# Attention over the memory by head pairs, with query and output pieces in twos

## The reference, cut to what matters

```python
def memory_cross_attention(h, mem_n, w_q, w_kv, w_o, qn, kn):
    q = rms_norm((h @ w_q).reshape(bsz, t, X_HEADS, X_HEAD_DIM), qn)      # 4 heads of 128
    kv = mem_n @ w_kv
    k = rms_norm(kv[..., :D_X].reshape(bsz, m, X_HEADS, X_HEAD_DIM), kn)
    v = kv[..., D_X:].reshape(bsz, m, X_HEADS, X_HEAD_DIM)
    s = jnp.einsum('bqhd,bmhd->bhqm', q, k).astype(jnp.float32) * (X_HEAD_DIM ** -0.5)
    prob = jax.nn.softmax(s, axis=-1).astype(v.dtype)
    o = jnp.einsum('bhqm,bmhd->bqhd', prob, v).reshape(bsz, t, D_X)
    return o @ w_o
```

## Time and profile before

| | before |
|---|---|
| median of 3 runs | 720.66 us (719.37 to 721.8) |
| profiled execution | 718.32 us, span 716.7 us |
| PE busy | 698.8 us, 98% of the span |
| DVE busy | 422.8 us, 59% |
| ACT busy | 308.2 us, 43% |
| chain that ended last | PE 83%, DVE 5%, POOL 4%, DMA 3%, ACT 3% |
| mean granted TensorE clock | 0.998 |

### The profile page before, as it was taken

One profiled execution on the slowest core, in us unless ns is written; L12 is line 12 of the kernel. 1 busy time (PEld: TensorE's weight loads), 2 busy tenths in 40 slices (PEclk: granted clock), 3 DMA queues, 4 the chain that ended last, 5 costly groups with the idle time before them and its releaser, 6 DMA issues.

```text
span 716.7 us, 10845 instructions
## 1 busy us (share of the span) xinstructions
PE 698.8 (98%) x3913; PEld 575.8 (80%) x3913; DVE 422.8 (59%) x711; ACT 308.2 (43%) x514; POOL 131.1 (18%) x134
## 2 busy tenths in 40 slices
PE   8999999999998999999999999999999999999998
PEld 7968887876776787878898888888888887888886
DVE  4997957737664657685856555554555574333333
ACT  5736344467753536253654334334333442332220
POOL 3999974033031110100200000000000000000000
PEclk9999999999999999999999999999999999999999
DMA  9645433167310033011124133232232332231303
GB/s 254 212 134 122 148 104 106 67 214 254 129 61 0 22 127 117 2 60 59 61 69 156 68 117 94 82 117 81 95 117 67 108 118 69 107 117 60 115 1 117
DMA packets 62999, 73.95 MB, mean 103 GB/s; under 512 B 20873, under 2 KB 47796, under 8 KB 62836
## 3 DMA queue, kind: packets, MB, share of 16 engines
q1 hardware_dynamic: 59172, 66.12, 28.8%
q10 hardware_dynamic: 3792, 7.36, 3.1%
HBM read 68.08 MB, written 5.78 MB: 103 GB/s over the span
## 4 chain that ended last, share of the span: by engine, by line
PE 83%; DVE 5%; POOL 4%; DMA 3%; ACT 3%; issue 1%; SPq 1%; DVEq 0%; POOLq 0%; ACTq 0%
PE pb L514 24%; PE pb L516 23%; PE pb L515 23%; PE pb L1769 8%; PE pb L1772 5%; POOL F L692 2%; DMA raw<-in_w_in 1%; DVE F L1253 1%; DVE wring L497 1%; DMA raw<-in_x_wkv 1%; ACT F L883 1%; DMA scr_y<-F 1%; ACT xs L883 1%; DVE xs L1259 1%; ACT wring L486 1%
## 5 line engine op out<-in xcount | busy, mean ns | idle before, releaser
L497 DVE TENSOR_TENSOR wring<-raw,wring 128x1024 fp32r<-128x1024 f32 x100 | 128.4, 1287 | 75.3 <-ACT wring L486 75.1
L514 PE MATMUL pb<-xs,wring 128*128 128x512 f32 (+1 forms) x448 | 165.4, 369 | 0.2 <-issue 0.2
L516 PE MATMUL pb<-xs,wring 128*128 128x512 f32 (+1 forms) x448 | 164.2, 366 | 0.0
L515 PE MATMUL pb<-xs,wring 128*128 128x512 f32 (+1 forms) x448 | 164.1, 366 | 0.0
L486 ACT ACTIVATE wring<-raw 128x1024 fp32r<-128x1024 f32 x100 | 105.0, 1053 | 86.6 <-PE pb L516 75.0
L1259 DVE SCALAR_TENSOR_TENSOR F<-pb,ccol,F 128x511 f32<-128x511 f32 x88 | 65.9, 749 | 103.4 <-ACT F L883 97.5
L514 PE MATMUL pb<-wring,bs 128*128 128x512 f32 x240 | 96.5, 402 | 1.9 <-ACT F L883 1.0
L514 PEld LDWEIGHTS pb<-xs,wring 128*128 128x128 f32 x448 | 84.5, 189 | 14.0 <-issue 0.6
L516 PEld LDWEIGHTS pb<-xs,wring 128*128 128x128 f32 x448 | 84.4, 188 | 13.9
L515 PEld LDWEIGHTS pb<-xs,wring 128*128 128x128 f32 x448 | 84.5, 189 | 13.2
L516 PE MATMUL pb<-wring,bs 128*128 128x512 f32 x240 | 93.7, 390 | 0.0
(11 more groups left out here) (142 smaller groups left out, 777.4 us busy)
## 6 DMA issues: line engine op xcount, KB each, us to landing
raw<-in_ffn_w_up SPq DMA_DIRECT2D x22, 1024.0 KB, 5.1
raw<-in_ffn_w_down SPq DMA_DIRECT2D x11, 1024.0 KB, 4.9
F<-in_x SPq DMA_DIRECT2D x8, 512.0 KB, 5.8
raw<-in_w_in ACTq DMA_DIRECT2D x4, 1024.0 KB, 5.9
raw<-in_w_out SPq DMA_DIRECT2D x4, 1024.0 KB, 5.0
raw<-in_w_in SPq DMA_DIRECT2D x3, 1024.0 KB, 5.8
raw<-in_x_wkv ACTq DMA_DIRECT2D x3, 1024.0 KB, 5.5
raw<-in_x_wq SPq DMA_DIRECT2D x2, 1024.0 KB, 5.2
```

The source lines that it names most:

```text
L497: ins = nc.vector.tensor_tensor(w_unit(u, 1), raw_unit(u), w_unit(u, 0).bitcast(f32), ALU.subtract)
L514: nc.tensor.matmul(ps, lh, rh, start=first, stop=False)
L515: nc.tensor.matmul(ps, lh, rl_, start=False, stop=False)
L516: return nc.tensor.matmul(ps, ll, rh, start=False, stop=last)
```

## The change

The 16 steps become 8 (`XP`), of two heads each. Both heads' scores stand in one bank (2 x 256 columns), one `row_max` gives two maxima, four probability transposes go to one bank, one `xp_evac` moves 512 columns. The exponentials stay one for each head. The query rows are no longer multiplied by their factor: raw rows are transposed, `row_max` multiplies its two maxima by `rs` (one small operation more), and the exponential takes `rs` as its scale. Query and output pieces are issued in twos, by the tables `XQ_AT` and `XO_AT` of PE's loop; weight unit XO+0 is split in step 1, XO+1 and XO+2 in step 2, XO+3 in step 4. `xo0` moves from bank 0 to bank 1. The lists of PE, ACT and DVE are rearranged:

```diff
-XO_AT = [4, 5, 6, 8]
+XQ_AT = {0: [(2, 1), (2, 2)], 1: [(2, 3), (3, 0)], 2: [(3, 1), (3, 2)], 3: [(3, 3)]}
+XO_AT = {4: [(0, 0), (0, 1)], 5: [(0, 2), (0, 3)], 6: [(1, 0), (1, 1)], 7: [(1, 2), (1, 3)]}
+XO_SPLIT_AT = {1: [0], 2: [1, 2], 4: [3]}
...
-        XO_BANK, W_BANK = (0, 2, 1, 7), (0, 1, 2, 0, 3, 1, 2, 3)
+        XO_BANK, W_BANK = (1, 2, 1, 7), (0, 1, 2, 0, 3, 1, 2, 3)
...
(ACT, x_probabilities)
-                drained(A_(pbuf[:, s % 2, 0:M], p[:, 0:M], ACT.Exp, bias=nmx[:, 32 + s:33 + s],
-                           accum_out=lsum[:, 32 + s:33 + s]), f"xs{s}")
+                for b in range(2):
+                    h = 2 * s + b
+                    c = EVC[f"qx{s // 2}"] + h % XH
+                    ins = A_(pbuf[:, h % 4, 0:M], p[:, b * M:(b + 1) * M], ACT.Exp, scale=rs[:, c:c + 1],
+                             bias=nmx[:, 32 + h:33 + h], accum_out=lsum[:, 32 + h:33 + h])
+                drained(ins, f"xs{s}")
...
(ACT, the loop)
+            for s in range(XP):
+                if s % 2 == 0:
+                    xp_evac(act, lambda o, i: A_(o, i, ACT.Copy), s)
+                if s + 1 < XP:
                     x_probabilities(s + 1)
+                if s in (1, 3):
+                    qx_rows(2 + s // 2)
+                if s == 7:
                     h_square("x3", "w", "x30", 0, 0)
+                if s in (3, 5, 7):
+                    xo_hi((s - 3) // 2)
+                for i in XO_SPLIT_AT.get(s, []):
+                    split_hi(act, U_XO + i)
...
(DVE)
             qx_event(0)
-            qx_rows(0)
+            transposed("qxt", qT, "x_qn", XD ** -0.5, [0])
+            root("qx0")
+            def row_max(s):
+                h, c = 32 + 2 * s, EVC[f"qx{s // 2}"] + 2 * s % XH
+                p = read(dve, f"xs{s}")
+                link(V.tensor_reduce(nmx[:, h:h + 2], p[:, :].rearrange("p (h m) -> p h m", h=2), AX.X, ALU.max,
+                                     negate=True))
+                tt(nmx[:, h:h + 2], nmx[:, h:h + 2], rs[:, c:c + 2], ALU.mult).then_inc(logit_ready, 1)
+
+            row_max(0)
+            transposed("qxt", qT, "x_qn", XD ** -0.5, [1])
             qx_event(1)
+            for s in range(XP):
+                if s in (1, 3, 5):
+                    root(f"qx{1 + s // 2}")
+                if s + 1 < XP:
                     row_max(s + 1)
+                if s % 2 == 1:
+                    xp_evac(dve, V.tensor_copy, s)
+                if s in (2, 4):
+                    transposed("qxt", qT, "x_qn", XD ** -0.5, [1 + s // 2])
+                if s in (2, 4, 6):
+                    t = s // 2 - 1
                     normalise(f"xpv{t}", 32 + XH * t, XH, XD, t)
+                if s in (2, 4):
+                    qx_event(1 + s // 2)
+                if s in (3, 5, 7):
+                    xo_lo((s - 3) // 2)
+                for i in XO_SPLIT_AT.get(s, []):
+                    split_lo(dve, U_XO + i)
+                if s == 6:
                     w_residual(0)
+                if s == 7:
                     x3_mean(0)
...
(PE)
             xq_piece(2, 0)
-            xq_piece(2, 1)
             x_scores(0)
-            x_scores(1)
+            qx_transposes(1)
+            for s in range(XP):
+                for t, i in XQ_AT.get(s, []):
+                    if (t, i) == (3, 0):
                         x2_ready(3)
+                    xq_piece(t, i)
+                for t, i in XO_AT.get(s, []):
+                    if i == 0:
+                        after_drain(pe, f"xo{t}")
+                    xo_piece(t, i)
+                if s + 1 < XP:
+                    x_scores(s + 1)
+                x_prob_transposes(s)
+                if s in (2, 4):
+                    qx_transposes(1 + s // 2)
                 if s >= 1:
                     x_values(s - 1)
+                if s in (3, 5, 7):
+                    xo_transposes((s - 3) // 2)
+            x_values(XP - 1)
```

More of the change, by code:

```diff
@@ L30 @@
 XH, XD = 4, 128
+XP = 4 * XH // 2
 DF = 2816
@@ L2038, in scores, with prob_transposes @@
                             filled(last, f"sc{s + b}")
[L2040 to L2043, removed]
-                    last = tr(p[:, a * 128:(a + 1) * 128], pbuf[:, s % ring, a * 128:(a + 1) * 128])
+            def prob_transposes(s, last_of_fill=True):
+                after_drain(pe, f"sc{s}")
+                p = fill(pe, f"pt{s}")
+                for a in range(s // H + 1):
+                    last = tr(p[:, a * 128:(a + 1) * 128], pbuf[:, s % 4, a * 128:(a + 1) * 128])
                 if last_of_fill:
-                    filled(last, f"{pre}{s}")
+                    filled(last, f"pt{s}")
             def values(s):
@@ L2072, in x_values @@
             def x_values(s):
[L2073 removed]
+                t = s // 2
                 after_drain(pe, f"xp{s}")
[L2075 to L2079 removed]
+                p = fill(pe, f"xpv{t}") if s % 2 == 0 else pb[uses[f"xpv{t}"][0]]
+                for b in range(2):
+                    at = slice((2 * s % XH + b) * XD, (2 * s % XH + b + 1) * XD)
+                    for a in range(MT):
+                        last = mm(p[:, at], ptb[:, s % 2, b * M + a * 128:b * M + (a + 1) * 128], xv[:, a, at],
+                                  a == 0, a == MT - 1)
+                if s % 2 == 1:
                     filled(last, f"xpv{t}")
@@ L2157, in _ @@
                     values(s - 3)
[L2158 removed]
+                prob_transposes(s, s != SS_AT)
                 if s == SS_AT:
@@ L2214, in qx_transposes, with x_prob_transposes @@
             def qx_transposes(t):
-                pe.wait_ge(xn_ready, NMK + t + 1)
+                after_drain(pe, f"qx{t}")
                 tile_transposes(f"qxt{t}", qk[:, t, :])
             def x_scores(s):
-                t, h = s // XH, s % XH
-                if h == 0:
+                t = s // 2
+                if s % 2 == 0:
                     after_drain(pe, f"qxt{t}")
                 p = fill(pe, f"xs{s}")
-                filled(mm(p[:, 0:M], qT[:, h, t * 128:(t + 1) * 128], kxT[:, h, :]), f"xs{s}")
+                for b in range(2):
+                    h = 2 * s % XH + b
+                    last = mm(p[:, b * M:(b + 1) * M], qT[:, h, t * 128:(t + 1) * 128], kxT[:, h, :])
+                filled(last, f"xs{s}")
+            def x_prob_transposes(s):
+                after_drain(pe, f"xs{s}")
+                p = fill(pe, f"xp{s}")
+                for b in range(2):
+                    for a in range(MT):
+                        last = tr(p[:, b * M + a * 128:b * M + (a + 1) * 128],
+                                  pbuf[:, (2 * s + b) % 4, a * 128:(a + 1) * 128])
+                filled(last, f"xp{s}")
             def xo_transposes(t):
```

75 lines of the change are left out of this document (6 added, 69 removed).

## The result

The changed kernel takes 731.57 us (median, 729.5 to 732.68) against 720.01 us of the kernel before in the same runs; the ratio is 1.016, 95% interval 1.0132 to 1.0187. The prediction was 731.3, in a range of 727.0 to 736.0. The profiled execution took 732.68 us, its span is 731.1 us.

The account below looks back on a forecast made before the run. PE, busy 98% of the span, bounds the kernel. New standstills of 13.2 us in place of 4.3 add 8.9, one clock fall 1.7: 10.6 on a median of 720.66 gives 731.3 us, range 727.0 to 736.0.

Parts of the forecast that it names:

- Removed waits: DVE's multiplication of the query rows (4 x 0.69) goes, and with it PE's wait before 290.65, 0.52 us.
- Row maximum of a pair: DVE's reduction of 512 columns: 0.69, with hand-over and small product 0.89 us, ends 0.6 and 1.05.
- A: Before the first output piece (0,0), PE waits for `xo0`'s low part, queued from values(1) on; standstill 5.8 us.
- B: Before piece (0,3), PE waits for XO+3's low part, behind the division of `xpv1` and `qx3`'s sums; standstill 2.7 us.
- C: Before piece (1,0), PE waits for `xo1`, whose high part stands behind pair 6's exponentials; standstill 1.9 us.
- D: Before piece (1,2), `w11` waits for bank 0, held by `w00` until DVE's residual behind `xpv2`'s division; standstill 1.9 us.
- E: Before piece (2,0), PE waits for `xo2`'s high and low parts, with values(7) as cover; standstill 0.9 us.
- the fifth rival: Pairs in one bank hold PE up through a bank read late, adding 1 to 3 us; chance 0.04.
- The clock: PE's granted clock falls once, to half, behind the longest standstill, costing 1.7 us, bounds 0 and 2.6.
- the second rival: Two or three clock falls, 1.7 or 3.4 us more: 733.0 or 734.7; chance 0.16.
- The third: Only A is real, B to E hide behind shifts of the lists: 722.2 us; chance 0.06.
- The fourth: New lists keep DVE ahead, its sums and splits run in free time, all standstill might go: 716.4 us; chance 0.04.

Follow-up runs that it names:

- the new lists: Changed kernel's pairs and factor in the exponential, with PE, ACT and DVE lists reordered and splits moved; 716.56 us, ratio 0.9962 to the kernel before.
- the repeat: The changed kernel run and traced once more, nothing altered; 731.86 us, ratio 1.0163 to the kernel before.
- pieces by ones: Against the new lists, output pieces of steps 4 to 7 issued singly, the second behind the step's transposes; 716.69 us, ratio 0.9973 to the kernel before.
- pairs in a good order: The new lists with the XO+2 split moved behind pair 4's exponentials on ACT and pair 5's row maximum on DVE; 715.6 us, ratio 0.9948.
- single heads in the best order that I tried: Kernel before with the factor in the exponential and the four XO weight splits one step earlier; 717.18 us, ratio 0.9978.
- the long gap filled: Changed kernel with six float32 matmuls on constants added on PE behind the transposes of `xo0`; 730.12 us, ratio 1.0143 to the kernel before.
- low part and rows first: Changed kernel with `xo0`'s high and low parts and the copy of `qx3`'s rows moved ahead of pair 4's work; 725.73 us, ratio 1.0073.
- `w11` in bank 5: Changed kernel with `w11` planned into bank 5 in place of bank 0; 729.15 us, ratio 1.0128 to the kernel before.

## Why the prediction was right

**Bound and lengths.** PE's count stayed and its standstills made the time. PE's work in the stretch was put at 45.3 us from 289.97 to the transposes of `xo3`. With no idle row left it is 45.5 (from 289.14, where the first query transposes stand, to 334.68), so of the 4.3 us of losses that were read off the kernel before, 4.0 could be won in that place.

**Removed waits.** The wait before the first query transposes went. Alone this part gave 0.55 us on the kernel before.

**Row maximum of a pair.** From its start at 316.62 to the exponential's at 317.62 it is 1.00 us with the hand-over, forecast 0.89 + 0.11, as taken. The exponentials behind it were longer than taken, as shown above.

**The chains.** A 5.8 forecast, 5.64 shown; B 2.7 and 2.38; C 1.9 and 1.97; D 1.9 and 1.72; E 0.9 and 0.59. The sum is 13.2 forecast against 12.3 shown; with what the idle rows leave out it is some 13.2 (an estimate from the 0.17 of chain A). In the stretch without slow clock: 65.3 - 55.9 = 9.4, forecast 8.9. The experiments show A and D one by one (D went with a bank, A went from 5.64 to 1.48 with the moves on two engines); B, C and E went only together with the rest, in the new lists, and were not cut by themselves.

**What the prediction had too simple.** Chain A was described as one chain. It had a twin through bank 0 (`qx3` to `w00`, 5.06 us when the first was cut), where the fifth rival saw only chain D's use of this bank, and POOL's power ran under the two splits (1.12 us came back when they were moved). Neither changed the time of this change. Both would have spoilt a forecast of its repair, and did spoil two of my expectations.

**The clock.** One fall of 1.7 was forecast. The first trace has one, of 1.86; the repeat has two, of 3.0 and 1.7. In the changed kernel's variants there were one or two falls, behind chain A, B or C. So the forecast stands in one of the two traces and the second rival (more falls; one sentence of the prediction calls it the third) in the other. How often each comes is not known. The Trainium skill, TensorE: Matmul & The Clock Gate, section "What's actually happening", calls the throttled state the default, which activity releases. The traces agree: where no gap over 1.5 us is left, the granted clock was 1.00 in the whole stretch in each of the six traces.

**Where luck helped.** The median came out 0.3 us from the forecast, but the difference between the two kernels was forecast as 10.6 us and measured as 11.6; the base of 720.66 was 0.65 us above what the kernel before took beside the changed one. And with one fall more in some executions than in others, no sum could promise a tenth of a microsecond.

**Two slips that did not decide.** The end of the second rival, 734.7, lies inside the stated range and not outside. And a step's parts sum to 2.48 with the prediction's own lengths (1.39 + 0.43 + 0.22 + 0.44), not to 2.45, so changes between kinds of matmul had 0.01 us each to give, not 0.04; the experiment with pieces by ones found none.

**The rivals.** The third (B to E hide) falls with four idle rows. The fourth (faster) was wrong for this order and right for its mechanism: with the sums of squares and the splits in DVE's free time the standstills do go, and the kernel is faster than before by 0.5%. The Trainium skill, Perfetto Trace Analysis, "Optimizing Scalar/DVE Operations", says that breaking instructions up may help where an unsaturated engine causes gaps. The runs limit what that says of this kernel: the gaps came from the order, and pairs in a good order (51.89 us) beat single heads in the best order that I tried (54.47), in one trace of each; the intervals of the two ratios overlap. Whether single heads in a list as carefully made would do as well was not tried.

## What to carry to other kernels

When the engine that bounds a kernel is full, a change of other engines' lists can only be judged by following, for each thing that it waits for, everything queued ahead on each engine, up to the last event that comes from the bound engine itself; the busy share of those engines says nothing. After the longest such wait is cut, look for its twin: a bank, a slow engine beside it, a hand-over that had been hidden. Put an operation whose input is late behind one whose result is due.

## What the runs showed of the hardware

- The clock fell in or behind standstills of PE of 4.6 to 5.65 us in all five traces that had one, but in some executions also behind 2.4 us (at 327.1 in the repeat, 330.1 with the long gap filled, 325.6 with low part and rows first) and 2.0 us (at 336.0 with `w11` in bank 5), and in others not behind the same ones. Each fall in the stretch cost 1.7 to 3.0 us. In one execution of the changed kernel the fall behind the 2.73 us before the pieces at 221, seen in all other traces, did not come.
- The same code before the stretch took 280.5 to 287.3 us in different executions, with idle rows of 0 to 3.3 us near 161 us and of 0.4 to 2.3 us near 177 us, and the clock at half behind some of them. Spans of two single profiles can differ by several us for that reason, and only a stretch with fixed ends tells what a local change did.
- A transpose or float32 matmul of 128 columns costs PE 0.11 us for each record (four in 0.44 to 0.45), one of 256 columns 0.21 (two in 0.43); a change between float32 and split matmuls costs nothing that a trace of this kernel can show (53.60 against 53.62 us with four more changes).
- An exponential of 256 columns that reads its scale from a tile takes ACT 0.56 us, one without 0.47, with single heads and with pairs.
- POOL's power of 128 x 4 values takes 1.01 us, and 1.9 where a weight split starts on DVE just behind its input, in each trace of the stretch.
